# Moving the down product of each expert behind that expert's own transposes, in a mixture-of-experts encoder

## The chip, the cores and the metric

One core of one Trainium2 chip runs the whole program. The metric is the time of one execution on the device in microseconds (us). TensorE does the matrix products and transposes (PE in the rows, PEld for its weight loads), VectorE (DVE), ScalarE (ACT) and GpSimd (POOL) the rest; SyncE (SP) only issues DMAs. All engines run their own programs at the same time and wait for each other by semaphores.

## The reference, cut to what matters

Two residual layers on x of 1024 tokens by 1024 features, in float32: layer 0 mixes tokens by a short convolution, layer 1 by latent attention. Each is followed by a mixture of experts, and that is the part that the change touches:

```
h = rms_norm(x)
each token picks its best group of 8, and in it its 2 best experts, with gates
for each of 64 experts e, over the tokens that picked it:
    hid = silu(h @ w_gate[e]) * (h @ w_up[e])     # 1024 -> 384
    y   = hid @ w_down[e]                         # 384 -> 1024
x = x + sum over the two picks of gate * y
```

## The kernel before, in words

The program has four phases: convolution, experts of layer 0, attention, experts of layer 1. `moe_phase` (from L873) is called for both expert phases. Tokens are sorted by expert into rounds: in a round every one of the 64 experts takes at most 64 of its rows. For these inputs one round does for all (128 experts are computed in the two phases).

**One expert on TensorE** has four steps. `turn_x` (L1228) transposes the gathered rows with four transposes (L1233). `gate_and_up` (L1236) makes both products with 32 matmul instructions (L1243), gate in the upper and up in the lower half of one PSUM bank. `turn_h` (L1248) transposes their copy with three transposes (L1252). `down` (L1256) is the down product, 12 instructions (L1262).

**Between the steps** other engines work. VectorE's `expert_x` (L1145) scales the transposed rows into `xT`. ScalarE's `copy_gate_up` (L1052) takes gate and up out of PSUM for `turn_h`; after it `make_silu` (L1058) takes the Silu of the transposed gate, and VectorE's `expert_h` (L1154) multiplies it with the transposed up to `hidden`, which `down` reads. ScalarE's `copy_y` (L1063) takes the down product out of PSUM, and POOL scatters it to the table `y_rows` in HBM (L1008, L1011). POOL also gathers the rows for `turn_x` (L998, L1001): the gather of expert g follows `turn_x(g - 2)`. Of each of `xT`, `gate_up`, `silu`, `hidden`, `y` and their PSUM banks there are two slots, used in turn.

**The order** is written out by hand, once for each engine. TensorE's `expert(g)` (L1276) runs `gate_and_up(g)`, `turn_x(g + 1)`, `down(g - 1)`, `turn_h(g)`. ScalarE's `expert(g)` (L1065) runs `copy_gate_up(g)`, `copy_y(g - 1)`, `make_silu(g)`. VectorE's runs `expert_x(g + 1)`, `expert_h(g)` (L1187, L1188).

**The weights** stream from HBM, 3 x 1536 KB for each expert. There are four slots for gate and up (two in the arena, two in the place of `hT`, named gate_up in the rows) and two for down. SyncE issues the loads in one loop (L960 to L966):

```
sp.wait_ge(gate_up_products, g + slot + done(0))
experts.load_gate_up(sp, slot, (g + slot + GU_SLOTS) % NE)
sp.wait_ge(y_products, g + slot + down_done(0))
experts.load_down(sp, slot % DOWN_SLOTS, (g + slot + DOWN_SLOTS) % NE)
```

Gate and up of expert g + 4 (L413) are issued once `gate_and_up(g)` is done, down of expert g + 2 (L417) once `down(g)` is. The loads of the first experts are issued before the phase begins (L450 to L459). The last two loads of down weights, of experts 62 and 63, follow behind the loop (L967). Once all y rows are stored, `y_rows` is loaded back, eight tiles (L976), and ScalarE (L1085) and VectorE (L1200, L1203) add both picks to x.

Of the kernel before, what the change touches and what calls it, by code (L numbers as in the profile page):

```python
# [30 lines left out]
NE, NG, EG = 64, 8, 8  # L31
# [15 lines left out]
GU_SLOTS, DOWN_SLOTS = 4, 2  # L47
# [825 lines left out]
def moe_phase(c, layer, last, experts):  # L873
# [65 lines left out]
    def done(g):  # L939
        return g + 1 + AHEAD  # L940

    def free(g):
        return g + 1

    def down_done(g):
        return g + 1 + DOWN_AHEAD
# [4 lines left out]
    def rounds(eng):  # L951
        eng.wait_ge(rounds_ready, 1)
        return eng.value_load(n_rounds[0:1, 0:1], min_val=1, max_val=MAXR)

    with nc.Block() as block:
# [86 lines left out]
        @block.scalar  # L1042
        def _(act):
            act.activation(c.exps[:, :, :, :], c.exps[:, :, :, :], ACT.Exp).then_inc(exp_out, 1)
            for s in (gate_up_copied, silu_ready, y_copied):
                act.sem_inc(s, AHEAD)
            count = rounds(act)

            def copy_gate_up(g, slot):
                act.wait_ge(gate_up_products, g + done(0))  # L1050
                act.wait_ge(h_turned, g + free(0))
                act.activation(gate_up[:, slot, :], c.ps[:, 2 + slot, 0:FF], ACT.Copy).then_inc(gate_up_copied, 1)  # L1052

            def make_silu(g, slot):
                act.wait_ge(h_turned, g + done(0))
                act.wait_ge(hidden_ready, g + free(0))
                turned = c.ps[:, 4 + slot, 0:FF].rearrange("p (j m) -> p j m", m=P)
                act.activation(silu[:, slot, :, :], turned[:, :, 0:RANKS], ACT.Silu).then_inc(silu_ready, 1)  # L1058

            def copy_y(g, slot):  # L1060
                act.wait_ge(y_products, g + down_done(0))
                act.wait_ge(y_stored, g + free(0))
                act.activation(y[:, slot, :], c.ps[:, 6 + slot, :], ACT.Copy).then_inc(y_copied, 1)  # L1063

            def expert(g, slot):  # L1065
                copy_gate_up(g, slot)
                copy_y(g - 1, 1 - slot)
                make_silu(g, slot)

            with act.Fori(0, count) as r:  # L1070
                g0 = r * NE
                copy_gate_up(g0, 0)
                make_silu(g0, 0)
                with act.Fori(0, NE // 2 - 1) as pair:
                    for n in (1, 2):
                        expert(g0 + pair * 2 + n, n % 2)
                expert(g0 + NE - 1, 1)
                copy_y(g0 + NE - 1, 1)

            act.wait_ge(gates_ready, 1)  # L1080
            for t in range(NT + (2 if norm else 0)):
                if t < NT:
                    act.wait_ge(y_pair_loaded[t % Y_RING], 16 * (t // Y_RING + 1))
                    first = y_pair[:, t % Y_RING, 0, :]
                    act.activation(first, first, ACT.Copy, scale=gates[:, 0, t:t + 1]).then_inc(first_scaled, 1)  # L1085
                if norm and 1 <= t < NT + 1:
                    act.wait_ge(x_added, t)
                    norm.act_squares(act, t - 1)
                if norm and t >= 2:
                    norm.act_rows(act, t - 2)  # L1090
# [122 lines left out]
        @block.tensor  # L1213
        def _(pe):
            for s in (x_turned, gate_up_products, h_turned):
                pe.sem_inc(s, AHEAD)
            pe.sem_inc(y_products, DOWN_AHEAD)
            pe.sem_inc(idx_products, 1)

            tok = c.ps[:, 0, :]  # L1220
            pe.matmul(tok, c.before[:, :], c.both[:, :, :].rearrange("p t e -> p (t e)"), start=True, stop=False)
            pe.matmul(tok, c.ones[:, :], earlier[:, 0:NT, :].rearrange("p t e -> p (t e)"),
                      start=False, stop=True).then_inc(counted, 1)
            pe.matmul(c.ps[:, 1, 0:NE], c.ones[:, :], earlier[:, NT, :], start=True, stop=True).then_inc(counted, 1)
            count = rounds(pe)
            pe.wait_ge(cleared, 1)

            def turn_x(g, slot):  # L1228
                pe.wait_ge(gather_done[slot], g * 8 + (16 - 8 * slot))
                pe.wait_ge(xT_ready, g + free(0))  # L1230
                rows = gathered[:, slot, :].rearrange("p (m j) -> p j m", j=4)
                for j in range(4):
                    last_ = pe.transpose(c.ps[:, slot, j * P:(j + 1) * P], rows[:, j, :], c.ident[:, :])  # L1233
                last_.then_inc(x_turned, 1)

            def gate_and_up(g, slot, w_slot):  # L1236
                pe.wait_ge(xT_ready, g + done(0))
                pe.wait_ge(w_gate_up_loaded[w_slot], g * 8 + (32 - 8 * w_slot))
                pe.wait_ge(gate_up_copied, g + free(0))
                for half in range(2):  # L1240
                    for j in range(4):
                        for i, row in enumerate((0, RANKS)):
                            last_ = pe.matmul(c.ps[row:row + RANKS, 2 + slot, 0:FF], xT[:, slot, j, half, :],  # L1243
                                              w_gate_up[w_slot][:, i, half, j * FF:(j + 1) * FF],
                                              start=(half + j == 0), stop=(half == 1 and j == 3))
                last_.then_inc(gate_up_products, 1)

            def turn_h(g, slot):  # L1248
                pe.wait_ge(gate_up_copied, g + done(0))
                pe.wait_ge(hidden_ready, g + free(0))  # L1250
                for j in range(KF):
                    last_ = pe.transpose(c.ps[:, 4 + slot, j * P:(j + 1) * P],  # L1252
                                         gate_up[:, slot, j * P:(j + 1) * P], c.ident[:, :])
                last_.then_inc(h_turned, 1)

            def down(g, slot):  # L1256
                pe.wait_ge(hidden_ready, g + done(0))
                pe.wait_ge(w_down_loaded[slot], g * 8 + (16 - 8 * slot))
                pe.wait_ge(y_copied, g + free(0))
                for j in range(KF):  # L1260
                    for half in range(2):
                        last_ = pe.matmul(c.ps[half * RANKS:(half + 1) * RANKS, 6 + slot, :], hidden[:, slot, j, :],  # L1262
                                          w_down[:, slot, j, half * BANK:(half + 1) * BANK],
                                          start=(j == 0), stop=(j == KF - 1))
                last_.then_inc(y_products, 1)

            with pe.Fori(0, count) as r:
                pe.wait_ge(onehot_ready, r + 1)
                for n in range(2 * NT):
                    last_ = pe.matmul(c.ps[:, 0, 0:2 * NE], onehot[:, n, :],  # L1270
                                      coded[:, n // NT, n % NT, :, :].rearrange("p a e -> p (a e)"),
                                      start=(n == 0), stop=(n == 2 * NT - 1))
                last_.then_inc(idx_products, 1)
                g0 = r * NE

                def expert(g, n):  # L1276
                    gate_and_up(g, n % 2, n % GU_SLOTS)
                    turn_x(g + 1, (n + 1) % 2)
                    down(g - 1, (n - 1) % 2)
                    turn_h(g, n % 2)  # L1280

                turn_x(g0, 0)
                gate_and_up(g0, 0, 0)
                turn_x(g0 + 1, 1)
                turn_h(g0, 0)
                with pe.Fori(0, NE // GU_SLOTS - 1) as turn:
                    for n in range(1, GU_SLOTS + 1):
                        expert(g0 + turn * GU_SLOTS + n, n)
                for e in range(NE - GU_SLOTS + 1, NE - 1):
                    expert(g0 + e, e)  # L1290
                gate_and_up(g0 + NE - 1, 1, GU_SLOTS - 1)
                down(g0 + NE - 2, 0)
                turn_h(g0 + NE - 1, 1)
                down(g0 + NE - 1, 1)
            if norm:
                for t in range(NT):
                    norm.pe_turn(pe, t)
# [606 lines left out]
```

## Time and profile before

| | |
|---|---|
| median of 3 runs | 2842.3 us (2840.99 to 2842.39) |
| the profiled execution, its own time | 2839.05 us |
| its span in the trace | 2837.3 us |
| mean granted clock of TensorE | 0.928 |
| TensorE busy | 2381.7 us, 84% |
| VectorE, ScalarE, GpSimd busy | 787.6, 640.9, 515.3 us |
| moved by DMA | 701.18 MB, mean 247 GB/s |

The span runs from the first to the last recorded event of one execution; its own time lies 1.75 us above it. "Idle before" is how long the engine stood still just before an instruction, with what released it; "issue" means that the profile shows no wait for that time. A granted clock of 1.00 is 2.4 GHz, 0.50 is 1.2 GHz. A DMA share of 1.00 means that all 16 DMA engines were busy. SPq rows are SyncE's issues of DMAs.

### The profile page before, as it was taken

How to read it: one execution, taken by the hardware profiler on the slowest of the kernel's cores; microseconds unless marked ns; L12 is line 12 of the kernel's file. 1: busy time of each engine (PE TensorE's matmuls, PEld its weight loads, DVE VectorE, ACT ScalarE, POOL GpSimd, SP SyncE). 2: the span in 40 equal slices, each digit the busy share in tenths (PEclk: the TensorE clock that was granted, in tenths of full speed). 3: DMA queues.
4: the chain of work that ended last, by engine and by line, in shares of the span. 5: the costliest groups of instructions: out<-in, count | busy, mean ns of one | idle time of the engine just before them, and what ended most of it. 6: DMA issues, size and time to landing. Idle time of an engine off the chain costs nothing. (4 is left out here: it accounts for less than half of the span.)

```text
span 2837.3 us, 35394 instructions
## 1 busy us (share of the span) xinstructions
PE 2381.7 (84%) x11822; PEld 1418.1 (50%) x11822; DVE 787.6 (28%) x2377; ACT 640.9 (23%) x1328; POOL 515.3 (18%) x775
## 2 busy tenths in 40 slices
PE   7999895888888888858699999989598888888873
PEld 5888672333333333335588888858333333333331
DVE  4222552000000000050666666625410000000003
ACT  3111220111111111141355555542111111111111
POOL 2222311212222222110111111122022212222210
PEclk9999997999999999979999999999699999999997
DMA  4111127999999999850000000100699999999996
GB/s 117 52 45 51 61 90 318 422 423 423 422 421 416 418 416 420 340 186 0 8 9 9 9 8 8 60 8 38 249 400 422 423 423 421 422 419 417 413 412 267
DMA packets 202298, 701.18 MB, mean 247 GB/s; under 512 B 36192, under 2 KB 65888, under 8 KB 202224
## 3 DMA queue, kind: packets, MB, share of 16 engines
q1 hardware_dynamic: 181744, 666.65, 58.1%
q0 software_dynamic: 20480, 33.64, 3.1%
q8 instruction: 35, 0.57, 0.1%
q14 instruction: 39, 0.32, 0.0%
HBM read 687.59 MB, written 46.14 MB: 259 GB/s over the span
## 5 line engine op out<-in xcount | busy, mean ns | idle before, releaser
L1262 PE MATMUL ps<-arena 128*64 128x512 f32 x1536 | 449.3, 730 | 222.5 <-issue 111.2
L1243 PE MATMUL ps<-arena 128*64 128x384 f32 x2048 | 349.9, 495 | 2.1 <-DVE arena L1145 2.1
L1262 PEld LDWEIGHTS ps<-arena 128*64 128x64 f32 x1536 | 127.0, 161 | 437.5 <-issue 314.4
L1243 PE MATMUL ps<-gate_up,arena 128*64 128x384 f32 x2048 | 344.4, 489 | 0.0
L1145 DVE TENSOR_TENSOR arena<-ps,xw 128x512 f32<-128x512 f32 x128 | 88.5, 691 | 687.8 <-PE ps L1233 687.8
L824 PE MATMUL ps<-hT_split,w_split 128*128 128x512 f32 x1152 | 264.3, 391 | 3.1 <-DVE hT_split L295 3.1
L824 PEld LDWEIGHTS ps<-hT_split,w_split 128*128 128x128 f32 x1152 | 216.9, 189 | 48.9 <-DVE hT_split L295 3.9
L1154 DVE TENSOR_TENSOR arena<-arena,ps 128x192 f32<-128x192 f32 x128 | 45.4, 354 | 698.7 <-ACT arena L1058 698.7
L1243 PEld LDWEIGHTS ps<-arena 128*64 128x64 f32 x2048 | 143.6, 138 | 177.0 <-issue 177.0
L1063 ACT ACTIVATE arena<-ps 128x512 f32<-128x512 f32 x128 | 76.5, 597 | 686.1 <-PE ps L1262 683.2
L1243 PEld LDWEIGHTS ps<-gate_up,arena 128*64 128x64 f32 x2048 | 141.1, 137 | 171.5 <-issue 171.5
L1052 ACT ACTIVATE arena<-ps 128x384 f32<-128x384 f32 x128 | 62.8, 491 | 631.1 <-PE ps L1243 631.1
L1008 POOL COPY col_idx<-scatter_idx 128x1 int32 (+1 forms) x128 | 23.4, 183 | 962.8 <-ACT arena L1063 962.8
L1001 POOL DMA_INDIRECT arena<-h_rows,col_idx x128 | 134.8, 1053 | 115.3 <-POOL col_idx L998 108.2
L1011 POOL DMA_INDIRECT y_rows<-arena,col_idx x128 | 131.8, 1030 | 113.2 <-POOL col_idx L1008 113.2
L1814 PE MATMUL ps<-arena 128*128 128x256 f32 x512 | 119.4, 388 | 7.4 <-ACT arena L1536 7.4
L1233 PEld LDWEIGHTS ps<-ident,arena 128*128 128x128 f32 x512 | 71.8, 209 | 94.9 <-issue 94.9
L1788 PE MATMUL ps<-k_split,q_split 128*128 128x512 f32 x384 | 114.0, 405 | 0.0
L1233 PE MATMUL ps<-ident,arena 128*128 128x128 f32 x512 | 96.5, 311 | 19.1 <-DMA arena<-h_rows,col_idx 19.1
L1814 PEld LDWEIGHTS ps<-arena 128*128 128x128 f32 x512 | 99.3, 195 | 22.8 <-issue 8.7
L1464 POOL TENSOR_TENSOR turned<-turned,minus_half 128x2 f32<-128x2 f32 x64 | 44.2, 690 | 354.3 <-ACT rows L1517 308.6
L1252 PEld LDWEIGHTS ps<-ident,arena 128*128 128x128 f32 x384 | 41.0, 144 | 123.4 <-issue 120.5
(203 smaller groups left out, 2926.9 us busy)
## 6 DMA issues: line engine op xcount, KB each, us to landing
arena<-in_exp_w_down SPq DMA_DIRECT2D x128, 1536.0 KB, 20.1
arena<-in_exp_w_gate SPq DMA_DIRECT2D x64, 1536.0 KB, 18.1
arena<-in_exp_w_up SPq DMA_DIRECT2D x64, 1536.0 KB, 24.3
gate_up<-in_exp_w_gate SPq DMA_DIRECT2D x64, 1536.0 KB, 18.8
gate_up<-in_exp_w_up SPq DMA_DIRECT2D x64, 1536.0 KB, 24.5
arena<-y_rows SPq DMA_DIRECT2D x16, 1024.0 KB, 10.9
arena<-in_conv_w_in SPq DMA_DIRECT2D x24, 512.0 KB, 3.5
h_rows<-rows SPq DMA_DIRECT2D x16, 512.0 KB, 2.7
```

What stands on the lines that cost most here:

```text
L824: last = pe.matmul(c.ps[:, 3 * h + j, :], w_split[:, j, a, k, :], hT_split[:, b, k, h * BANK:(h + 1) * BANK], start=(k == 0 and a == b), s ...
L1001: pool.indirect_dma_start(gathered[:, slot, :], None, h_halves, bass.IndirectOffsetOnAxis(ap=col_idx[:, slot, :], axis=0), bounds_check=2 ...
L1011: pool.indirect_dma_start(y_halves, bass.IndirectOffsetOnAxis(ap=col_idx[:, 2 + slot, :], axis=0), y[:, slot, :], None, bounds_check=4 * S ...
L1052: act.activation(gate_up[:, slot, :], c.ps[:, 2 + slot, 0:FF], ACT.Copy).then_inc(gate_up_copied, 1)
L1063: act.activation(y[:, slot, :], c.ps[:, 6 + slot, :], ACT.Copy).then_inc(y_copied, 1)
L1145: dve.tensor_tensor(xT[:, slot, :, :, :].rearrange("p j h m -> p (j h) m"), c.ps[:, slot, :].rearrange("p (a m) -> p a m", m=RANKS), bc(c. ...
L1154: dve.tensor_tensor(hidden[:, slot, :, :], silu[:, slot, :, :], turned[:, :, RANKS:P], ALU.mult).then_inc(hidden_ready, 1)
L1233: last_ = pe.transpose(c.ps[:, slot, j * P:(j + 1) * P], rows[:, j, :], c.ident[:, :])
L1243: last_ = pe.matmul(c.ps[row:row + RANKS, 2 + slot, 0:FF], xT[:, slot, j, half, :], w_gate_up[w_slot][:, i, half, j * FF:(j + 1) * FF], st ...
L1262: last_ = pe.matmul(c.ps[half * RANKS:(half + 1) * RANKS, 6 + slot, :], hidden[:, slot, j, :], w_down[:, slot, j, half * BANK:(half + 1) * ...
L1788: pe.matmul(out, q_split[:, a, 0, q], k_split[:, par, 2 * b, keys], start=(n == 0), stop=False)
L1814: last = pe.matmul(c.ps[:, 7, 0:2 * P], v[:, par, kt, :], probsT[:, j % 2, kt, :], start=(kt == 0), stop=(kt == NT - 1))
```

## The change

On TensorE, `expert(g)` now runs `gate_and_up(g)`, `turn_x(g + 1)`, `turn_h(g)`, `down(g)`: the down product follows the transposes of the same expert, where before it was that of the expert before. ScalarE's `copy_y` moves with it: `copy_gate_up(g)`, `make_silu(g)`, `copy_y(g)`. The special first and last steps of both loops go away. VectorE's, POOL's and SyncE's programs stay as they are, as do all semaphores, the values waited for and the number of slots.

```diff
--- before.py
+++ after.py
@@ -1064,18 +1064,14 @@
 
             def expert(g, slot):
                 copy_gate_up(g, slot)
-                copy_y(g - 1, 1 - slot)
                 make_silu(g, slot)
+                copy_y(g, slot)
 
             with act.Fori(0, count) as r:
                 g0 = r * NE
-                copy_gate_up(g0, 0)
-                make_silu(g0, 0)
-                with act.Fori(0, NE // 2 - 1) as pair:
-                    for n in (1, 2):
-                        expert(g0 + pair * 2 + n, n % 2)
-                expert(g0 + NE - 1, 1)
-                copy_y(g0 + NE - 1, 1)
+                with act.Fori(0, NE // 2) as pair:
+                    for slot in range(2):
+                        expert(g0 + pair * 2 + slot, slot)
 
             act.wait_ge(gates_ready, 1)
             for t in range(NT + (2 if norm else 0)):
@@ -1273,25 +1269,19 @@
                 last_.then_inc(idx_products, 1)
                 g0 = r * NE
 
-                def expert(g, n):
+                def expert(g, n, last_one=False):
                     gate_and_up(g, n % 2, n % GU_SLOTS)
-                    turn_x(g + 1, (n + 1) % 2)
-                    down(g - 1, (n - 1) % 2)
+                    if not last_one:
+                        turn_x(g + 1, (n + 1) % 2)
                     turn_h(g, n % 2)
+                    down(g, n % 2)
 
                 turn_x(g0, 0)
-                gate_and_up(g0, 0, 0)
-                turn_x(g0 + 1, 1)
-                turn_h(g0, 0)
                 with pe.Fori(0, NE // GU_SLOTS - 1) as turn:
-                    for n in range(1, GU_SLOTS + 1):
+                    for n in range(GU_SLOTS):
                         expert(g0 + turn * GU_SLOTS + n, n)
-                for e in range(NE - GU_SLOTS + 1, NE - 1):
-                    expert(g0 + e, e)
-                gate_and_up(g0 + NE - 1, 1, GU_SLOTS - 1)
-                down(g0 + NE - 2, 0)
-                turn_h(g0 + NE - 1, 1)
-                down(g0 + NE - 1, 1)
+                for e in range(NE - GU_SLOTS, NE):
+                    expert(g0 + e, e, e == NE - 1)
             if norm:
                 for t in range(NT):
                     norm.pe_turn(pe, t)
```

## Rows read from the trace of the kernel before

**Rows 1.** Slices of the span on the page: what the DMA engines moved
```profile
GB/s 117 52 45 51 61 90 318 422 423 423 422 421 416 418 416 420 340 186 0 8 9 9 9 8 8 60 8 38 249 400 422 423 423 421 422 419 417 413 412 267
```

**Rows 2.** Windows: us, busy time per engine, granted clock, DMA share, GB/s
```profile
500.00:1200.00 700.00, 590.53 (x2993) 240.69 (x2991) 61.34 (x117) 77.34 (x177) 142.93 (x231) 0.93 1.00 413
```

**Rows 3.** Costliest groups on the page: busy, mean ns, idle before
```profile
L1262 PE MATMUL ps<-arena 128*64 128x512 f32 x1536 | 449.3, 730 | 222.5 <-issue 111.2
```

**Rows 4.** Chain that ended last: start us, us, what
```profile
2185.09 18.95 DMA arena<-in_exp_w_down
2204.08 4.49 PE ps L1262 x12
```

**Rows 5.** Timeline, first phase, experts without a wait: start us, us, instruction
```profile
486.96 0.55 PE L1252 MATMUL ps<-ident,arena 128*128 128x128 f32 x3
487.44 5.38 PE L1243 MATMUL ps<-gate_up,arena 128*64 128x384 f32 x32
...
492.75 0.75 PE L1233 MATMUL ps<-ident,arena 128*128 128x128 f32 x4
492.94 0.49 ACT L1052 ACTIVATE arena<-ps 128x384 f32<-128x384 f32 x1 [5.05 <-PE ps L1243]
493.43 2.79 PE L1262 MATMUL ps<-arena 128*64 128x512 f32 x12
493.53 0.69 DVE L1145 TENSOR_TENSOR arena<-ps,xw 128x512 f32<-128x512 f32 x1 [5.25 <-PE ps L1233]
496.15 0.55 PE L1252 MATMUL ps<-ident,arena 128*128 128x128 f32 x3
```

**Rows 6.** Timeline, four down products after gaps of different length
```profile
522.17 2.79 PE L1262 MATMUL ps<-arena 128*64 128x512 f32 x12 [1.10 <-DMA arena<-in_exp_w_down]
...
1145.73 4.42 PE L1262 MATMUL ps<-arena 128*64 128x512 f32 x12 [2.49 <-DMA arena<-in_exp_w_down]
...
2420.52 2.79 PE L1262 MATMUL ps<-arena 128*64 128x512 f32 x12 [2.27 <-issue]
...
2759.27 5.39 PE L1262 MATMUL ps<-arena 128*64 128x512 f32 x12 [3.59 <-issue]
```

**Rows 7.** Timeline, TensorE at the end of both expert phases
```profile
1195.10 4.19 PE L1262 MATMUL ps<-arena 128*64 128x512 f32 x12 [4.19 <-DMA arena<-in_exp_w_down]
...
1207.58 0.55 PE L1252 MATMUL ps<-ident,arena 128*128 128x128 f32 x3
1209.04 2.80 PE L1262 MATMUL ps<-arena 128*64 128x512 f32 x12 [0.91 <-DVE arena L1154]
...
2783.51 2.79 PE L1262 MATMUL ps<-arena 128*64 128x512 f32 x12 [3.17 <-DMA arena<-in_exp_w_down]
...
2796.05 2.80 PE L1262 MATMUL ps<-arena 128*64 128x512 f32 x12 [0.91 <-DVE arena L1154]
```

**Rows 8.** Timeline, start of both phases: issues of loads, VectorE's first product
```profile
466.89 0.39 SPq L413 DMA_DIRECT2D arena<-in_exp_w_gate  x1
...
470.19 0.35 DVE L1154 TENSOR_TENSOR arena<-arena,ps 128x192 f32<-128x192 f32 x1 [2.06 <-ACT arena L1058]
...
478.06 0.37 SPq L417 DMA_DIRECT2D arena<-in_exp_w_down  x1
...
2057.35 0.35 DVE L1154 TENSOR_TENSOR arena<-arena,ps 128x192 f32<-128x192 f32 x1 [2.06 <-ACT arena L1058]
...
2065.23 0.37 SPq L417 DMA_DIRECT2D arena<-in_exp_w_down  x1
```

**Rows 9.** Windows: first phase's start, a down product, second phase's end
```profile
476.00:477.00 1.00, 1.00 (x8) 0.38 (x6) 0.00 (x0) 0.00 (x0) 0.00 (x0) 1.00 0.53 201
...
479.00:480.00 1.00, 1.00 (x10) 0.46 (x8) 0.16 (x1) 0.00 (x0) 0.19 (x1) 1.00 0.51 66
...
2205.00:2206.00 1.00, 1.00 (x6) 0.29 (x4) 0.00 (x0) 0.00 (x0) 0.00 (x0) 0.50 1.05 438
...
2781.00:2786.00 5.00, 2.50 (x12) 0.77 (x12) 0.15 (x1) 0.00 (x0) 0.00 (x0) 1.00 0.13 52
```

## The prediction

> Notation: for expert g, GU(g) is the gate and up product (L1243), TX(g) the four transposes of its gathered rows (L1233), TH(g) the three transposes of gate and up (L1252), Y(g) the down product (L1262); W(g) is the 3.1 MB of gate and up weights, D(g) the 1.6 MB of down weights.
>
> **What bounds the kernel now.** I read the slices of the page first: in the two expert phases, over half of the span, the DMA engines move 412 to 423 GB/s in every slice inside a phase [rows 1]. Then a long stretch inside the first phase: DMA share 1.00 at 413 GB/s, TensorE at a mean granted clock of 0.93 [rows 2]. Then the costliest group: TensorE stands still for 222.5 us in front of Y, 111.2 of it put down to "issue" [rows 3], the rest almost all to the down weights; both names follow one another in one pattern, so I take both as waits for D. The chain of waits says the same: from the end of Y(g), which frees D's slot, 18.95 us pass until the reloaded slot has landed for Y(g+2) [rows 4]. With the DMA engines full, that time is queueing, not latency. Y of expert 5 starts at 522.17, Y of expert 61 at 1195.10 [rows 6, 7]: 672.9 us over 56 experts, 12.02 us each, and that is the pace of the weight stream. The reader should see a saturated stream with a TensorE that waits about 1.8 us per expert.
>
> **The steady state after the change.** TensorE's cost of one expert without a wait stands in [rows 5]: GU to TX 492.75 - 487.44 = 5.31, TX to Y 0.68, Y to TH 496.15 - 493.43 = 2.72, TH to the next GU 487.44 - 486.96 = 0.48; together 9.2. In the new order TX follows GU as now, but TH(g) then needs ScalarE's copy of gate and up. That copy starts 0.19 after TX (492.94) and takes 0.49, so TH can start about 0.07 later, 6.06 after GU began; TX covers the copy but for that. TH then runs 0.55, to 6.61. Y(g) next needs Silu and the product on VectorE, which nothing covers any more. The trace has that bare chain once in each phase, at its last expert: TH from 1207.58 for 0.55, then Y at 1209.04, released by VectorE's product after a gap of 0.91 [rows 7]. VectorE's work for TX(g+1), 0.69 long and starting 0.78 after TX [rows 5], ends 6.78 after GU began, before its product for TH is due at about 7.1, so it adds nothing. Y starts 6.61 + 0.91 = 7.52 after GU and the next GU 2.72 later: 10.24 us per expert instead of 9.2. The 1.04 us more per expert is costed at nothing, because 12.02 - 10.24 = 1.78 us of waiting for weights still covers it. Were that cover gone, 112 experts in both phases would cost 1.04 x 112 = 116 us.
>
> The moved step issues no DMA itself, but its end releases one. SyncE's program is unchanged: W(g+4) after GU(g), then D(g+2) after Y(g). Before, Y(g) ended after GU(g+1), so D(g+2) and W(g+5) went out together; now W(g+5) goes out about 5.3 us after D(g+2). The order in the queue is the same, and at the end of Y(g) the same D(g+1) and W(g+4), 4.7 MB or some 11 us of work, still lie in it. I cost that at nothing. ScalarE's y copy moves behind Silu: it waits for Y(g) and is over (0.60) long before GU(g+1) ends. On POOL's queue the scatter of g waits for that copy and has TX's next gather behind it; Y(g) now comes before TX(g+2), not after, so nothing there is later. Both cost nothing.
>
> **The head of each phase.** The stream has one hole now. W(4) is issued at 466.89 and has been moved by about 476.5 (share 0.53 in 476 to 477, [rows 9]); D(2) is issued only at 478.06, after GU(1) and Y(0), and data flow again from about 480.0, 2.0 after the issue (share 0.51, 66 GB/s in 479 to 480) [rows 8, 9]. Afterwards Y(0) starts when the product of expert 0 is ready: 470.19 + 0.35, and 0.06 for the signal, is 470.6. D(2) goes out 3.0 later, 473.6, and is in the queue before W(4) is through; it is moved until 476.5 + 1.573 MB / 0.42 = 480.25. GU(1) runs from 473.3 to 478.6, W(5) is issued at 478.95 (0.33 after, as W(4) was) and moves from 480.95. Before, W(5) could move from 480.0 + 3.75 = 483.8. The stream is 2.85 us ahead. The second phase gives the same: product at 2057.35, so GU(1) ends at 2065.8 and W(5) moves from 2068.1; before, D(2) was issued at 2065.23 and W(5) moved from 2067.2 + 3.75 = 2070.95 [rows 8]. Gain 2 x 2.85 = 5.7 us; bounds: 0 (a hole elsewhere eats it) and 2 x 3.5, the whole hole.
>
> **The tail of each phase.** Let S be the time at which D(61) has landed, the last transfer that comes out of a full queue. At S the old order has GU(62) and TX(63) behind it; Y(61), TH(62), GU(63), Y(62), TH(63), Y(63) remain, and Y(63) ends 2796.05 + 2.80 - 2783.51 = 15.34 after S in the second phase, 1209.04 + 2.80 - 1195.10 = 16.74 in the first, where Y(61) ran for 4.19 [rows 7]. The new order has at S only TH(61) behind it: Y(61) 2.72, a whole GU-to-Y of expert 62 (7.52), Y(62) 2.72, another 7.52 for expert 63, Y(63) 2.80, together 23.28. That is 7.94 more per phase, 15.9 in both, on the path: what follows (scatter, the load of y rows, the sum) waits for Y(63). Bounds: 7.94 is the least if the clock holds; a Y(61) at low clock adds 1.4 to 1.7 to the second phase; if D(61) finds TensorE late nothing is lost beyond that.
>
> **Sum.** +15.9 - 5.7 = +10.2 us. The profiled execution took 2839.05 us with a span of 2837.3; it would take 2849.3. The median of the runs is 2842.3, 3.3 above; I give the forecast on the median: **2852.5 us**. With the bounds (8.9 to 17.6 more) the likeliest case has its own range of 2851 to 2860.
>
> **A rule that speaks against the change.** First the rows: after a gap of 1.10 or 2.27 us Y ran in 2.79, after 2.49 in 4.42 [rows 6], so somewhere beyond two microseconds the clock falls from 2.4 to 1.2 GHz (the granted clock is 0.50 from 2205 to 2206, in the Y that began at 2204.08 after a wait) [rows 4, 9]. The new order joins its 0.91 of chain to the wait for weights, a gap of 0.91 + 1.78 = 2.7 per expert instead of 1.8 + 0.0. A Y in low clock costs 4.42 - 2.79 = 1.63 more; the expert then takes 10.24 + 1.63 = 11.87, still under 12.02, and after it the next gap is only 0.91 to 1.1, which keeps the clock. By the rows the sum stays. The Trainium skill, "TensorE: Matmul & The Clock Gate", section "HAM oscillation — how this bites in real kernels", says that a loop which waits for a DMA between its bursts of matmuls starts every burst throttled; if that held for each expert here and for longer than Y, TensorE would become the bound, which is the first rival.
>
> **Rivals.**
> 1. *TensorE becomes the bound through the clock* (also slower, but by much more). It decides once low clock costs over 1.78 us per expert. For it: gaps grow, and a few Y now take 5.39 (one after a gap of 3.59 us) [rows 6]. Against: such a loss shortens the next gap. If each Y took 5.39, an expert would take 10.24 + 2.6 = 12.84, 0.82 more, 92 us in 112 experts: about 2945. A mild form, a third of it: 2883. Chance 0.08.
> 2. *The 18.95 us is latency after all* (not slower, but faster). Two slots then give a period of (18.95 + 4.49) / 2 = 11.7 [rows 4]; freeing the slot after a Y of 2.80 gives 10.9, 0.85 less, 95 us less in 112 experts: about 2757. It decides if the DMA engines have idle time in the steady state. For it: the chain of waits runs through exactly this loop. Against: share 1.00 over 700 us and no slice inside a phase below 412 GB/s [rows 1, 2]. Chance 0.04.
> 3. *The stream ends earlier by about what the tail costs* (no measurable change). At the end of the second phase the share is 0.13, two engines of sixteen, from 2781 to 2786 while TensorE waits for D(61) [rows 9]: two engines lag by several us, and S is theirs. If the more even issue lets them catch up by 4 us more per phase, the time is 2852.5 - 8 = 2844.5; by the full 7, 2838.5. Against: they never lack work, so nothing in the issue can make them faster. Chance 0.14. The Trainium skill, "DMA: Bandwidth & Descriptors", section "Latency and other measured facts", says that two of the engines are usually slower, probably through descriptors that POOL issues; the change leaves the number of those alone, so by it this rival falls.
>
> **How the numbers follow.** Forecast 0.74, rivals 0.08, 0.04 and 0.14. A measurement of this kernel can tell about 0.2%, 5.7 us, from no change. Slower by more than that: the forecast and rival 1, less a little for a head gain larger or a tail smaller than worked out: 0.77. Within: most of rival 3 and that remainder: 0.15. Faster: rival 2 and the far end of rival 3: 0.08. The range of 8 in 10 reaches down into rival 3 and up past the bounds to the mildest form of rival 1: 2843 to 2868.
>
> **What would show it.** Right: Y(5) to Y(61) still 12.0 us per expert; DMA share 1.00 there; gaps before Y near 2.7 on average with none under 0.9; no hole at 477 to 480; Y(63) ending about 23.3 after Y(61) began. Wrong: experts at clearly over 12.1 us with gaps of 0.91 (rival 1); under 11.9 (rival 2); S over 5 us earlier from the phase's first GU than before (rival 3); or a new hole in the DMA stream inside the phase, which would say that the later issue of W matters.

## The result and the profile after

| | before | after |
|---|---|---|
| median, us | 2841.64 of 4 runs (2838.81 to 2842.39) | 2864.44 of 4 runs (2858.64 to 2865.77) |
| profiled execution, us | 2839.05 | 2858.64 |
| its span, us | 2837.3 | 2856.9 |

The ratio is 1.0072, with a 95% interval of 1.006 to 1.0084: the change makes the kernel slower by 0.7%, 22.8 us between the medians (20.5 by the ratio) where the forecast was 10.2, or 10.9 against the median of the table. The profiled execution is the fastest of its four; it shows 19.6 us. The ratios, here and below, leave out two executions far above the rest, one of the kernel before (3079.3 us) and one of e6 (5993.87 us); the medians count them.

The page of the kernel after, its slices of DMA traffic, then groups of instructions (busy, mean ns, idle before), the last from the list of ScalarE's; they answer to [rows 1] and [rows 3]:

```profile
GB/s 116 52 44 57 54 99 330 422 422 423 421 418 420 420 409 420 295 184 0 8 9 9 9 8 8 59 8 38 272 402 420 421 423 423 422 420 420 410 388 234
...
L1258 PE MATMUL ps<-arena 128*64 128x512 f32 x1536 | 455.9, 739 | 164.4 <-DVE arena L1150 149.9
...
L1052 ACT ACT_TABLE_LOAD x64 | 82.1, 1283 | 343.9 <-PE ps L1239 343.9
...
L1248 PE MATMUL ps<-ident,arena 128*128 128x128 f32 x384 | 70.0, 291 | 82.6 <-ACT arena L1052 82.6
...
L1058 ACT ACT_TABLE_LOAD x64 | 82.1, 1283 | 1.1
```

The weights still stream at the same rate: from 500 to 1200 the DMA share is 1.00 at 413 GB/s and the granted clock 0.93, all three as in [rows 2]. But the wait in front of the down product (L1258, L1262 before) is no longer one for weights: of 164.4 us, 149.9 end with VectorE's product. And there are two groups that the kernel before had only at the head of each phase (two loads in each group): ScalarE loads an activation table 64 times in front of the copy of gate and up and 64 times in front of Silu. TensorE stands still for 82.6 us until that copy is there. The change has a second edit that the prediction read only as a reordering: ScalarE's loop now starts with the first expert, and begins with a Copy.

Two experts of the second phase, timeline of the kernel after (start us, us, instruction, idle before):

```profile
2266.77 2.80 PE L1258 MATMUL ps<-arena 128*64 128x512 f32 x12 [0.81 <-DVE arena L1150]
...
2274.84 1.28 ACT L1052 ACT_TABLE_LOAD   x1 [4.62 <-PE ps L1239]
...
2276.13 0.49 ACT L1052 ACTIVATE arena<-ps 128x384 f32<-128x384 f32 x1
2276.64 1.28 ACT L1058 ACT_TABLE_LOAD   x1
2276.67 0.55 PE L1248 MATMUL ps<-ident,arena 128*128 128x128 f32 x3 [1.27 <-ACT arena L1052]
...
2278.70 4.29 PE L1258 MATMUL ps<-arena 128*64 128x512 f32 x12 [1.48 <-DVE arena L1150]
```

In the odd expert (the first line) the chain is the forecast one, with a gap of 0.81 (0.91 forecast). In the even one two table loads of 1.28 stand in it. The first holds up the copy, and TH waits 1.27; the second, in front of Silu, lies partly beside TH and leaves a gap of 1.48 before Y, in other experts 1.67. From Y to Y that is 2278.70 - 2266.77 = 11.93; an expert without loads takes 9.98 where the Y before it ran at full clock (expert 63 of the second phase, 2805.77 to 2815.75). And the Y after the two gaps ran in 4.29, at low clock (granted clock 0.50 from 2278.70 to 2281.70).

### The profile page after: what moved, and what is told of

Same layout as the page of the kernel before. It is cut to its first block and busy times, and to the rows that moved or that the text cites. A ratio compares the mean times of both kernels' runs of the same rounds, so it can differ in the third digit from the quotient of the medians.

```text
span 2856.9 us, 35554 instructions
## 1 busy us (share of the span) xinstructions
PE 2380.4 (83%) x11822; PEld 1448.5 (51%) x11822; DVE 787.9 (28%) x2377; ACT 813.2 (28%) x1452; POOL 513.2 (18%) x775
## 5 line engine op out<-in xcount | busy, mean ns | idle before, releaser
L1258 PE MATMUL ps<-arena 128*64 128x512 f32 x1536 | 455.9, 739 | 164.4 <-DVE arena L1150 149.9
L1258 PEld LDWEIGHTS ps<-arena 128*64 128x64 f32 x1536 | 126.6, 163 | 392.5 <-issue 246.6
L1239 PEld LDWEIGHTS ps<-arena 128*64 128x64 f32 x2048 | 163.6, 140 | 195.8 <-issue 147.7
L1239 PEld LDWEIGHTS ps<-gate_up,arena 128*64 128x64 f32 x2048 | 151.1, 139 | 202.3 <-issue 196.0
L1052 ACT ACT_TABLE_LOAD x64 | 82.1, 1283 | 343.9 <-PE ps L1239 343.9
L1248 PE MATMUL ps<-ident,arena 128*128 128x128 f32 x384 | 70.0, 291 | 82.6 <-ACT arena L1052 82.6
L1229 PEld LDWEIGHTS ps<-ident,arena 128*128 128x128 f32 x512 | 71.9, 209 | 94.2 <-issue 94.2
L1229 PE MATMUL ps<-ident,arena 128*128 128x128 f32 x512 | 96.5, 312 | 18.3 <-DMA arena<-h_rows,col_idx 18.3
L1512 ACT ACTIVATE rows<-ps,turned 128x1024 f32<-128x1024 f32 x64 | 71.4, 1115 | 137.2 <-DVE turned L1682 137.2
## 6 DMA issues: line engine op xcount, KB each, us to landing
arena<-y_rows SPq DMA_DIRECT2D x16, 1024.0 KB, 10.9
```

Source lines behind the costliest of these rows:

```text
L1248: last_ = pe.transpose(c.ps[:, 4 + slot, j * P:(j + 1) * P], gate_up[:, slot, j * P:(j + 1) * P], c.ident[:, :])
```

## Where the time lies in the two executions

I set each phase's zero at the start of its first TX and read TensorE's timeline (first phase, second phase):

| us from TX(0) | before | after |
|---|---|---|
| Y(5) starts | 65.9, 64.7 | 71.7, 71.3 |
| Y(61) starts | 738.8, 740.1 | 737.4, 738.9 |
| Y(63) ends | 755.5, 755.4 | 763.8, 763.6 |
| pace, Y(5) to Y(61) | 12.02, 12.06 | 11.89, 11.92 |
| Y over 3.5 us, of 64 | 28, 25 | 28, 29 |

So the phases are 8.3 and 8.1 us longer, and all of it lies behind Y(61), which comes 1.4 and 1.2 us earlier. The other 3 us of this pair of executions lie in code that the change does not touch: from Y(63) to the next phase's TX(0) 831.6 before and 834.1 after, and 830 to 839.5 in the kernels below, so a single execution cannot say more about them.

The pace of 11.9 has two halves. From Y(5) to Y(33) the kernel after takes 11.72 us per expert in both phases (11.96 and 11.99 before), and nearly every gap before Y is that of the chain, 0.81, 1.48 or 1.67: there TensorE sets the pace. From Y(33) to Y(61) it takes 12.05 and 12.12 (12.08 and 12.13 before), and longer gaps come in, up to 2.78: it has caught up with the stream.

## The experiments

"Head" is the start of a phase, "tail" its last three experts. All ratios are to runs of the kernel before on the same chip, whose medians were 2841.3 to 2842.1.

| kernel | median, us | ratio, 95% interval |
|---|---|---|
| after | 2864.44 | 1.0072 (1.006 to 1.0084) |
| e1: after, no table load in the loop | 2857.62 | 1.0058 (1.0044 to 1.0071) |
| e2: before, table loads in the loop | 2842.56 | 1.0007 (0.9997 to 1.0016) |
| e3: before, experts 0 to 3 in the new order | 2843.34 | 1.0003 (0.9994 to 1.0012) |
| e4: before, experts 61 to 63 in the new order | 2859.37 | 1.0061 (1.0049 to 1.0073) |
| e5: e1, experts 61 to 63 in the old order | 2848.57 | 1.0026 (1.0015 to 1.0036) |
| e6: e3, Silu table loaded early | 2837.61 | 0.9982 (0.9973 to 0.9991) |
| e7: after, last pair of experts without table loads | 2859.35 | 1.0058 (1.0044 to 1.0071) |
| e8: before, Silu table loaded early | 2842.64 | 1.0003 (0.9993 to 1.0014) |
| e9: new order throughout, no table load on its path | 2854.25 | 1.0039 (1.0025 to 1.0053) |

**e1_peeled: the table loads taken out of the loop.**

```diff
-                with act.Fori(0, NE // 2) as pair:
-                    for slot in range(2):
-                        expert(g0 + pair * 2 + slot, slot)
+                expert(g0, 0)
+                with act.Fori(0, NE // 2 - 1) as pair:
+                    for n in (1, 2):
+                        expert(g0 + pair * 2 + n, n % 2)
+                expert(g0 + NE - 1, 1)
```

> The changed kernel, but ScalarE's first and last expert stand outside its loop, so that the loop holds no load of an activation table. Theory A (the 124 table loads that the change put into the loop made TensorE the bound, by 1.97 us in every second expert and low clock after it): without them an expert takes 9.97 us on TensorE, the stream bounds again at 12.0, what is left is 2 x 7.4 in the tails minus 2 x 2.85 in the heads: about 2851 us, +9. Theory B (the order itself costs it, through longer gaps and a lower clock; the table loads lie in time that TensorE waits anyway): 2860 to 2866 as the changed kernel.

The table loads are gone from the loop, and the median falls by 6.8 us. By the ratios it is 4.0 us, and the two intervals overlap, so the runs alone hardly tell; the traces do, in the tail (e7 below). The fall is less than theory A wanted (2851): 15.5 us over the kernel before stay. The loads do not explain most of the loss.

**e2_before_tables: the same loads in the old order.**

```diff
                 make_silu(g0, 0)
+                act.wait_ge(silu_ready, g0 + done(0))
+                act.activation(silu[:, 1, 0, 0:1], silu[:, 0, 0, 0:1], ACT.Exp)
                 with act.Fori(0, NE // 2 - 1) as pair:
```

> The kernel before, with one Exp on ScalarE between its first expert and its loop, so that its loop too loads both tables once per two experts. Theory A (in the old order down(g-1) stands between the copy and the transposes that need it, and covers the loads): no change, 2842 us, within 2. If a table load costs its own time wherever it stands: 64 x 2.56 = up to 160 us more.

Its loop loads both tables once per two experts, as the changed one does, and it costs nothing that can be told. Timeline of e2:

```profile
699.18 1.28 ACT L1052 ACT_TABLE_LOAD   x1 [5.04 <-PE ps L1245]
...
700.47 0.49 ACT L1052 ACTIVATE arena<-ps 128x384 f32<-128x384 f32 x1
...
707.37 0.55 PE L1254 MATMUL ps<-ident,arena 128*128 128x128 f32 x3
```

The copy is done at 700.96, and TH that needs it comes 6.4 us later, behind Y of the expert before. So a load of 1.28 us is free there, and so is Silu's (708.18 to 709.46), which lies beside the next GU (from 707.84). In the new order TH follows at once.

**e3_new_head and e4_new_tail: the new order at one end only.** e3 runs experts 0 to 3 as `gate_and_up`, `turn_x`, `turn_h`, `down` and goes over to the old order at expert 4; e4 has the old order up to `turn_h(61)` and the new one from there. TensorE's part of e4 (ScalarE's follows the same order):

```diff
-                for e in range(NE - GU_SLOTS + 1, NE - 1):
-                    expert(g0 + e, e)
-                gate_and_up(g0 + NE - 1, 1, GU_SLOTS - 1)
-                down(g0 + NE - 2, 0)
-                turn_h(g0 + NE - 1, 1)
-                down(g0 + NE - 1, 1)
+                expert(g0 + NE - 3, NE - 3)
+                down(g0 + NE - 3, 1)
+                for e in range(NE - 2, NE):
+                    gate_and_up(g0 + e, e % 2, e % GU_SLOTS)
+                    if e < NE - 1:
+                        turn_x(g0 + e + 1, (e + 1) % 2)
+                    turn_h(g0 + e, e % 2)
+                    down(g0 + e, e % 2)
```

> The kernel before, with the new order for experts 0 to 3 only, old order after. Theory A: the hole in the weight stream at the start of each phase is closed and the end of the stream moves up by 2.85 us per phase, nothing else changes: about 2836.6 us, 5.7 less. Rival (the stream is not what sets the end, or the hole comes back later): 2842, no change.

> The kernel before, with the new order for experts 61 to 63 only. Theory A: after Y(61) two whole experts stand instead of one and a half: 2 x 7.4 = 14.8 us more, about 2857. Rival (part of the tail lies beside the late weights of experts 62 and 63, or beside the scatter): clearly less, 2842 to 2850.

The tail alone costs 17.3 us, more than the 15.5 left in e1, and 2.5 more than expected. Its timeline has both Y(61) at low clock, 5.39 and 4.41 long for 4.19 and 2.80 before, after waits of 9.7 and 9.2 for the weights: Y(61) to the end of Y(63) takes 25.6 and 24.3 us, in e1 24.1 and 22.8. The head alone gives nothing, where 5.7 were expected. Its timeline says why:

```profile
468.38 0.55 PE L1256 MATMUL ps<-ident,arena 128*128 128x128 f32 x3 [1.26 <-ACT arena L1052]
470.42 5.39 PE L1266 MATMUL ps<-arena 128*64 128x512 f32 x12 [1.49 <-DVE arena L1158]
```

Y(0) starts at the forecast time, 470.4, but runs in 5.39 instead of 2.79: D(2) and after it W(5) are issued about 2.5 us later than forecast. The kernel after does the same (gaps of 1.27 and 1.67). Windows of it, the holes that stay in the stream and then the clock during Y(0) (columns as in [rows 9]):

```profile
476.00:477.00 1.00, 1.00 (x8) 0.46 (x6) 0.00 (x0) 0.39 (x1) 0.18 (x1) 0.94 0.08 31
...
482.00:483.00 1.00, 0.36 (x3) 0.12 (x2) 0.80 (x2) 0.33 (x1) 0.18 (x1) 1.00 0.67 98
...
471.00:474.00 3.00, 3.00 (x10) 0.98 (x8) 0.00 (x0) 0.00 (x0) 0.00 (x0) 0.50 0.99 412
```

The granted clock is 0.50 from 471 to 474, after two gaps with 0.55 of transposes between them. One hole became two, at 476 and from 482. Those gaps come of expert 0's own two table loads, which stand in the kernel before as well. There the first holds up TH(0) just the same (a gap of 1.26 at 468.57), but GU(1) follows TH(0) at once and covers the second.

**e6_head_table and e8_before_table: the table loaded early.**

```diff
             act.activation(c.exps[:, :, :, :], c.exps[:, :, :, :], ACT.Exp).then_inc(exp_out, 1)
+            act.wait_ge(exp_out, 1)
+            act.activation(silu[:, 1, 0, 0:NG], c.exps[:, 0, 0, 0:NG], ACT.Silu)
             for s in (gate_up_copied, silu_ready, y_copied):
```

> As e3_new_head (new order for experts 0 to 3), but ScalarE loads the Silu table before the phase's first expert, by a Silu of 8 columns ahead of it. Theory C (the gain of the head was lost since both table loads of expert 0, 1.27 and 1.67 us of gap around 0.55 of transposes, put TensorE at 1.2 GHz from 469 to 476): clock stays up, D(2) is issued at about 471.6, W(5) at about 477, the stream has no hole, 2 x 3.5 us less than before: about 2835. Rival (the end of the stream is not set by its start): 2842.

> The kernel before, with the Silu table loaded ahead of the phase's first expert, as in e6_head_table, and nothing else. It tells how much of e6_head_table's 5 us less is the early load alone. Theory C: TH(0) comes 1.26 us earlier and D(2) with it, the hole in the stream shrinks from 3.5 to 2.2 us: 2 x 1.3 = 2.5 us less, about 2839; the other half of e6_head_table's gain is the new order of the first experts. Rival (the early load is all of it): 2836 to 2837.

e6 is 3.7 us faster than the kernel before between the medians, 5.1 by the ratio (2.6 to 7.7), and its interval excludes 1: the one version that beats both. e8, the early load alone, gives nothing that can be told, where 2.5 were expected. So neither the new order of the first experts (e3) nor the early load does it alone: the gain is that order, once its clock holds. The window of e6 that holds the place of the hole (same columns):

```profile
470.00:486.00 16.00, 15.03 (x85) 6.31 (x87) 1.15 (x3) 2.01 (x4) 4.68 (x7) 1.00 1.00 409
```

The granted clock and the DMA share are both 1.00 over these 16 us. Of 7.0 us expected, 5.1 came.

**e5_old_tail: the new order with the old tail.** As e1, with `down(61)` behind `gate_and_up(62)` and `turn_x(63)`, and the old order from there.

> As e1_peeled (new order, no table load in ScalarE's loop), but experts 61 to 63 in the old order. Theory A (what is left of the loss in e1_peeled, 15.5 us, is the tail alone): back to 2842 to 2844. Rival (the new order also costs time in the steady state, through low clock): 2848 or more.

7.3 us stay, so by its expectation the steady state would cost something. The timeline shows another reason, of the experiment's own making. Timeline of e5, end of the second phase:

```profile
2773.66 4.22 PE L1266 MATMUL ps<-arena 128*64 128x512 f32 x12 [2.98 <-DMA arena<-in_exp_w_down]
2777.71 5.33 PE L1247 MATMUL ps<-arena 128*64 128x384 f32 x32
...
2784.50 5.38 PE L1247 MATMUL ps<-gate_up,arena 128*64 128x384 f32 x32 [0.24 <-DVE arena L1149]
...
2790.49 2.80 PE L1266 MATMUL ps<-arena 128*64 128x512 f32 x12
```

Going over from new to old puts two GU between Y(60) and Y(61). Y(61) starts 16.83 after Y(60) and without a wait: TensorE comes to it later than its weights do. From TX(0) Y(61) comes at 739.8 and 742.5 in the two phases, in e1 at 736.6 and 739.2. So about 3 us are lost per phase against e1, which would be some 6 of the 7.3; these are single executions, and the split of the 7.3 is argued from them, not measured. e5 does not show a cost in the steady state, and e1 speaks against one: its Y(61) comes 2.2 and 0.9 us earlier than that of the kernel before.

**e7_tail_peeled: only the tail's table loads away.**

```diff
-                with act.Fori(0, NE // 2) as pair:
+                with act.Fori(0, NE // 2 - 1) as pair:
                     for slot in range(2):
                         expert(g0 + pair * 2 + slot, slot)
+                for slot in range(2):
+                    expert(g0 + NE - 2 + slot, slot)
```

> The changed kernel, but ScalarE's last two experts stand outside its loop, so that no table is loaded in the tail; the other 62 pairs of loads stay. Theory D (the loads cost time only where no wait for weights covers them, in the tail): 2 x 1.97 = 3.9 us less than the changed kernel, about 2860.5, within 1 or 2 of e1_peeled's 2857.6. Rival (they make TensorE the bound all along): no change against the changed kernel's 2864.4 beyond 1 us.

5.1 us less than the changed kernel between the medians, 4.0 by the ratios, and the same ratio as e1, which has no table loads in the loop at all. The intervals reach some 4 us to either side, so the ratios alone do not settle it; the traces add to them. From the start of Y(61) to the end of Y(63) the kernel after takes 26.4 and 24.7 us, e7 24.4 and 22.8, e1 24.1 and 22.8. Ahead of the tail, Y(61) comes at 737.4 and 738.9 in the kernel after and at 736.6 and 739.2 in e1. So the four loads of the tail cost their time, 2 us per phase, and no cost of the other 120 shows.

**How near the bound lies: three kernels without the stream's down weights.** They leave out the reloads of down weights; all experts use those of experts 0 and 1. Each is one execution.

```diff
-                    sp.wait_ge(y_products, g + slot + down_done(0))
-                    experts.load_down(sp, slot % DOWN_SLOTS, (g + slot + DOWN_SLOTS) % NE)
...
-                pe.wait_ge(w_down_loaded[slot], g * 8 + (16 - 8 * slot))
+                pe.wait_ge(w_down_loaded[slot], 16)
```

> The kernel before without its reloads of down weights (D(0) and D(1) serve all experts, wrong weights): TensorE's own pace in the old order. From the rows of before: 9.2 us per expert, no Y in low clock but at the start; if POOL's or ScalarE's work sets the pace instead, more.

> The changed kernel without its reloads of down weights: D(0) and D(1) are used for all experts (wrong weights), so the stream carries 3.1 MB per expert, some 7.9 us, and TensorE's own pace shows. From the rows of the changed kernel: 9.97 and 11.94 us in turn with the clock up, 10.96 on average; with low clock in every second down product 11.8 to 11.9. If the pace is under 11, the 11.9 of the changed kernel is the weights' pace, if it is 11.8 or more, TensorE's.

> e1_peeled without its reloads of down weights: TensorE's own pace in the new order without table loads. From the rows of the changed kernel: 9.97 us per expert, gaps of 0.81 before every Y, and the clock up throughout, since no gap is over 1 us. If gaps of 0.81 in every expert are enough for low clock: 10.8 or more.

| TensorE's own pace, Y(5) to Y(61), first phase | us per expert | Y over 3.5 us, of 64 | time, us |
|---|---|---|---|
| n1: old order | 9.19 | 0 | 2523.9 |
| n3: new order, no table loads in the loop | 10.02 | 1 | 2633.4 |
| n2: new order as changed | 11.65 | 27 | 2836.1 |

In the window from 500 to 1000 TensorE is busy throughout in n1. The same window of n3 and then of n2, columns as in [rows 2]:

```profile
500.00:1000.00 500.00, 457.62 (x2546) 196.48 (x2543) 52.26 (x100) 70.87 (x150) 121.77 (x200) 1.00 0.88 339
```

```profile
500.00:1000.00 500.00, 424.30 (x2204) 176.35 (x2201) 44.96 (x86) 114.94 (x171) 105.81 (x174) 0.94 0.76 291
```

n1 came out at 9.19 and n3 at 10.02 (9.98 in the second phase), where 9.2 and 9.97 had been read from the rows. n2 at 11.65 lies between the two values that its expectation set apart: the changed kernel's TensorE has 0.4 us per expert left against a stream of 12.02, where the prediction gave it 1.78. Of the 1.63 between n3 and n2, half of 1.97 is table loads and the rest the low clock that their gaps bring: gaps of 0.81 before each Y kept the clock at 1.00 in n3, gaps of 1.27 and 1.48 with 0.55 between them gave 27 Y at low clock in n2.

**e9_no_tables: the order alone.** e1 and the early Silu together.

> The new order for all experts, with no table load left beside it: ScalarE's first and last expert outside its loop as in e1_peeled, and the Silu table loaded ahead of the first expert as in e6_head_table. Theory E (the sum of the prediction was right but for the table loads): heads 2 x -2.85, tails 2 x 7.9, about 2851. Rival (the new order costs something in the steady state too, as e5_old_tail's 7.4 us may say): 2856 or more.

12.7 us between the medians, 11.1 by the ratio (7.1 to 15.1), a median between the two expectations: the order without its table loads costs what the sum said (10.2), within what these runs can tell.

## Why the prediction was right or wrong

The direction and the range were right: slower, 2864.4 in 2843 to 2868. The size was not: 22.8 us (20.5 by the ratio) for 10.2 of the sum, and the likeliest case's own range, 2851 to 2860, missed it. That the wide range holds it is luck in part: its top was put there for a mild form of rival 1, not for table loads, which stand in no case of the prediction.

- **The step that failed is the one on ScalarE: "ScalarE's y copy moves behind Silu", with "Both cost nothing".** The copy itself costs nothing. But the same hunk takes ScalarE's first expert into the loop, and with that 124 table loads. The diff showed the first expert's removal, and the first product of a phase in [rows 8], 470.19, held two such loads already; I did not look at ScalarE's instructions there. Taken out of the loop, and with expert 0's own out of the head (e9), the loads give back about 10 us, and e9's interval lies clear of the changed kernel's. Of these, 4 to 5 lie in the tail by e7 and 3 to 5 in the head (e9 against e1); each of the two is the difference of kernels whose intervals overlap.
- **The head** was forecast at -5.7. The time of Y(0) was right (470.6 forecast, 470.4), its clock was not: Y(0) at 1.2 GHz took 5.39, D(2) went out at 475.98 for 473.6 and W(5) at 481.38 for 478.95, a hole stayed, and the gain was given back (e3, nothing). The forecast had no low clock in this step; it read from [rows 8] when the product of expert 0 comes and not which gaps lie ahead of it. With the clock up it is there (e6, -5.1).
- **The tail** was forecast at +15.9 and measured at +17.3 alone (e4), with Y(61) at low clock in both phases, which the forecast had among its bounds. From Y(61) to the end of Y(63), 23.3 forecast, the new order took 24.1 and 22.8 without the loads (e1). In the kernel after that stretch took 26.4 and 24.7. Its first phase:

```profile
1194.48 2.80 PE L1258 MATMUL ps<-arena 128*64 128x512 f32 x12 [0.81 <-DVE arena L1150]
...
1204.39 0.55 PE L1248 MATMUL ps<-ident,arena 128*128 128x128 f32 x3 [1.27 <-ACT arena L1052]
1206.43 4.49 PE L1258 MATMUL ps<-arena 128*64 128x512 f32 x12 [1.48 <-DVE arena L1150]
...
1218.10 2.80 PE L1258 MATMUL ps<-arena 128*64 128x512 f32 x12 [0.81 <-DVE arena L1150]
```

  The first line answers to Y(61) in [rows 7]. Expert 62 has the table loads (1.97 more) and a Y at low clock (1.7 more; 2.80 in the second phase), expert 63 neither: its TH, with no TX ahead of it, waits 0.67 for the copy, where 0.75 were forecast.
- **The steady state** was costed at nothing, and it cost nothing that can be seen: Y(61) came 1.4 and 1.2 us earlier, not later. That was right with less reserve than I thought: the kernel after began 6 us late at Y(5) and caught up at TensorE's own pace. The signs named for it did not come: Y waits for VectorE, not for weights, in 61 and 60 of 64 experts, and the gaps are 0.81 and 1.48 or 1.67 in turn, 1.3 on average, not 2.7. Without the loads they are 1.8 and 1.9 on average (e9), with 28 and 29 of 64 Y at low clock. I had named such gaps at over 12.1 us per expert as the mark of the first rival, and a pace under 11.9 as that of the second; 11.89 touches that mark, but by the catching up and with the DMA share at 1.00.
- **The reading of the clock was wrong.** I took it from [rows 6] that it falls somewhere beyond two microseconds of gap and that gaps of 0.91 to 1.1 keep it. The length of the gap before Y does not decide: [rows 7] itself has a Y of 2.79 after 3.17, and the kernel before one after 3.19 (at 2698.16), while in e1 a single gap of 1.75 (at 1025.08) and in most even experts of the kernel after two gaps, of 1.27 and 1.48 or 1.67, were followed by low clock. What does decide stays open.
- **Rival 1** (TensorE the bound through the clock) was half right in its mechanism, and came to no price: TensorE does set the pace in the first half of each phase, at 11.72 us, and n2 shows low clock at work, at 11.65 us per expert just under the stream. The rule of the Trainium skill, "TensorE: Matmul & The Clock Gate", section "HAM oscillation — how this bites in real kernels", was weighed for waits on a DMA; here other engines' chains of 1.3 and 1.5 us did it, in 27 of the 32 experts that have them in n2's first phase, so the trace agrees for most bursts, not for every one.
- **Rivals 2 and 3** fall. The stream's pace did not change. Two engines of sixteen lag at its end as before (DMA share 0.13 before and 0.12 after, from 738 to 742 us after the second phase's TX(0)). When D(61) landed in the kernel after, the trace does not tell; Y(61), released by VectorE in both phases, came 1.4 and 1.2 us earlier, and not 4.

## What to carry to other kernels

An edit that moves work into a hardware loop can change what is loaded inside the loop: here one Copy and one Silu taken into ScalarE's loop (the change), or one Exp put ahead of it (e2), gave two table loads in every turn, and taking the first expert out (e1) removed them. That the table at the loop's entry decides is my inference from these three. So look at which table is surely there at the entry, and look for table loads in the rows of the first turn, before costing such an edit at nothing. A chain through three engines that is bare of cover costs little while a stream bounds the kernel, but all of it in the tail, where the stream no longer covers anything; so the order that is best for the head of a phase (product out early, slot free early) and for its tail (work done ahead of the last load) can differ, and e6 takes the new one only for the first experts.

## What the runs showed of the hardware that I had not expected

Two gaps of 1.27 and 1.48 us with 0.55 us of transposes between them put TensorE at 1.2 GHz in most cases (27 Y at low clock in n2's first phase, where 32 of 64 experts have these gaps), while single gaps of 0.81 in every expert kept it at 2.4 GHz (n3, granted clock 1.00). For other single gaps no length parts the two: 1.10, 2.27 and 3.19 kept the clock in the kernel before, 1.75 in e1 did not. An activation table load took 1.28 us each time, 64 of them 82.1 us.
